# A language-model forward pass in one kernel: three buffers get other addresses modulo 256 bytes

## The reference

```python
def swiglu(x, w_gate, w_up, w_down):
    return (jax.nn.silu(x @ w_gate) * (x @ w_up)) @ w_down
# layer 0: rms_norm, w_in, RWKV-7 recurrence beside sparse attention, w_out, network 0
# layer 1: network 1, then gated linear attention beside forgetting attention, network 2
# layer 2: network 3, then attention over a latent with a top-64 choice, network 4
# then a last rms_norm
```

## The kernel before

| buffer | rounded operands in it | start mod 256, before | after |
|---|---|---|---|
| x, xn | | 128 | 128 |
| uT, yT | uT_h, uT_l | 64 | 128 |
| ffb | h_r | 128 | 128 |
| inh | in_h | 128 | 192 |
| ring | ring_r | 128 | 192 |
| cst (constants), misc | | 128 | 192 |
| wk | w_gu, w_dn, even_h, odd_h, out_h | 128 | 192 |

## Time and profile before

### The profile page before, as it was taken

How to read it: one execution, slowest core, us unless ns; L and a number is a source line. 1 busy time by engine, 2 the same in 40 slices (tenths; PEclk the granted TensorE clock), 3 DMA queues, 4 the chain that set the end, 5 groups by cost and what they waited for, 6 DMA issues and landing times. The chain is left out here.

```text
span 1418.8 us, 25483 instructions
## 1 busy us (share of the span) xinstructions
PE 1390.2 (98%) x10044; PEld 1289.4 (91%) x10044; DVE 945.5 (67%) x1539; ACT 690.5 (49%) x1107; POOL 82.7 (6%) x137
## 2 busy tenths in 40 slices
PE   8999999999999999999999999999999999999997
PEld 7897988999989999999989999999999988899997
DVE  5778567766668666667467666676665676676665
ACT  6764446443354344376654443443443756643342
POOL 1030010000020000010000000100000123000000
PEclk9999999999999999999999999999999999999999
DMA  9344006654536555523356544365555423465540
GB/s 362 141 154 186 2 6 239 219 190 177 184 128 223 192 201 184 179 95 133 130 195 224 201 181 178 134 223 190 202 185 179 149 90 135 178 223 182 191 160 30
DMA packets 33069, 239.47 MB, mean 169 GB/s; under 512 B 6864, under 2 KB 13280, under 8 KB 14304
## 3 DMA queue, kind: packets, MB, share of 16 engines
q1 hardware_dynamic: 30320, 234.84, 45.7%
q10 hardware_dynamic: 2672, 3.58, 0.7%
HBM read 236.15 MB, written 2.25 MB: 168 GB/s over the span
## 5 line engine op out<-in xcount | busy, mean ns | idle before, releaser
L501 PE MATMUL ps<-uT_h,w_gu 128*128 128x256 f32 x3520 | 618.4, 281 | 2.5 <-ACT uT_h L1319 2.5
L501 PEld LDWEIGHTS ps<-uT_h,w_gu 128*128 128x128 f32 x3520 | 538.4, 188 | 12.6 <-issue 5.1
L501 PE MATMUL ps<-uT_l,w_gu 128*128 128x256 f32 x1760 | 482.0, 281 | 0.0
L501 PEld LDWEIGHTS ps<-uT_l,w_gu 128*128 128x128 f32 x1760 | 331.7, 192 | 0.0
L501 PE MATMUL ps<-w_dn,h_r 128*128 128x512 f32 x1320 | 317.9, 390 | 0.4 <-DVE h_r L2073 0.3
L1371 ACT CAST w_gu<-ring 128x2048 fp32r<-128x2048 f32 x110 | 210.0, 1909 | 155.4 <-PE ps L501 154.4
L501 PEld LDWEIGHTS ps<-w_dn,h_r 128*128 128x128 f32 x1320 | 239.8, 188 | 45.2 <-issue 1.8
L2031 DVE TENSOR_TENSOR w_gu<-ring,w_gu 128x2048 fp32r<-128x2048 f32 x110 | 252.1, 2292 | 35.4 <-ACT w_gu L1371 35.4
L2064 DVE TENSOR_TENSOR us<-ps,bc 128x256 f32<-128x256 f32 x110 | 46.5, 423 | 201.9 <-PE ps L501 201.9
L1384 ACT ACTIVATE wk<-wk 128x256 f32<-128x256 f32 x110 | 46.0, 418 | 266.5 <-DVE wk L2062 266.4
L1377 ACT CAST w_dn<-ring 128x1024 fp32r<-128x1024 f32 x110 | 115.8, 1053 | 75.7 <-PE ps L501 75.5
(11 more groups left out here) (398 smaller groups left out, 1695.7 us busy)
## 6 DMA issues: line engine op xcount, KB each, us to landing
ring<-wstream SPq DMA_DIRECT2D x144, 1536.0 KB, 6.5
cst<-consts_in SPq DMA_DIRECT2D x1, 2185.0 KB, 13.7
wk<-t_row ACTq DMA_DIRECT2D x1, 2048.0 KB, 8.1
wk<-masks_in SPq DMA_DIRECT2D x1, 1216.0 KB, 24.2
x<-x_in SPq DMA_DIRECT2D x2, 512.0 KB, 5.0
ring<-wstream SPq DMA_DIRECT2D x1, 1024.0 KB, 9.1
inh<-gains ACTq DMA_DIRECT2D x2, 512.0 KB, 9.8
tri_blocks<-wk SPq DMA_DIRECT2D x3, 256.0 KB, 2.8
```

Source lines behind the costliest of these rows:

```text
L501: return pe.matmul(o, l, r, start=start, stop=stop, skip_group_check=True)
```

## The change

Buffers get other places. The pad of 192 bytes ahead of uT goes; ffb moves from behind the ring to behind yT; a pad of 64 bytes stands ahead of inh in place of the one of 64 bytes that stood there. All buffers from inh on thus change their start modulo 256 by +64, and so do uT and yT. No instruction, loop, wait or transfer is added or removed.

```diff
         x = sb("x", [P, TT, D])
         xn = sb("xn", [P, TT, D])
-        sb("phase_up", [P, 48])
         uT = sb("uT", [P, KC, T])
         yT = sb("yT", [P, KC, T])
-        sb("phase_down", [P, 16])
+        ffb = sb("ffb", [P, 4, T])
+        sb("phase_inh", [P, 16])
         inh = sb("inh", [P, KC * 3 * P])
         gb = inh[:, 0:2 * D].rearrange("p (a b) -> p a b", b=D)
         sb("gate_r", [P, 2 * KC * 24])
         ring = sb("ring", [P, RING, SLOT])
-        ffb = sb("ffb", [P, 4, T])
         cst = sb("cst", [P, NCONST])
```

## The result

The changed kernel takes 1402.56 us (median of 4 runs, 1401.33 to 1405.57) against 1418.22 us (4 runs, 1417.04 to 1421.44): ratio 0.9889, 95% interval 0.9876 to 0.9902. It is 15.7 us faster, where 4 us slower was forecast. The profiled execution has a span of 1401.6 us against 1418.8.

A forecast was written before the change was run, and what follows sets the result against it. TensorE, busy for 98% of the span, was taken to bound the kernel. The down product's 3.0 us plus 0.6 us for dear first matmuls, 3.6 us on the median 1418.63, gave 1422.2 us, range 1399 to 1430.

The forecast's parts named there:

- The down product's price: Down product's 1,320 512-column matmuls: relation going from 0 to -64 costs 2.25 ns each, 3.0 us.
- the 0.6 for first matmuls that stay a little dear: Down product: first matmuls after each switch stay dear, some 5 ns a step over 110 steps, 0.6 us.
- Both entries are slow. So I leave gate/up at 117.7 ns, cost nothing.: Gate/up after the down product: two handovers from -64 to +64 read slow, so spacing stays 117.7 ns, 0 us.
- gate/up goes fast: Gate/up product: the new down product leaves it at fast spacing, 21.6 us back, 1400.6 us; chance 0.20.
- The fear that absolute position counts: Gate/up's 5,280 matmuls: if absolute position modulo 256, not the difference, counts, each nanosecond is 5.3 us.
- nothing changes: TensorE's two reads: they do not disturb each other, so the time stays 1418.6 us; chance 0.15.
- pays in full: Down product: all 12 matmuls at 232 ns each step, +7.0 us, 1425.6 us; chance 0.20 including other losses.
- The small pairs at 0: Ten groups, 312 matmuls, pairing a staying buffer with a moving one: at most 1.3 us either way, taken as 0.

The follow-up runs named there:

- e13: e6 with the last down matmul cut from 512 to 384 columns; 1412.53 us, ratio 0.9956.
- e12: e6 with the last down matmul cut from 512 to 256 columns; 1388.23 us, ratio 0.9782.
- e1: Changed kernel's activation and weight positions modulo 256, but inner values at 192, so the down product is at relation 0 again; 1418.17 us, ratio 0.9994.
- e2: Activations and weights where the kernel before has them modulo 256, inner values at 64, so the down product is at relation -64; 1405.82 us, ratio 0.9916.
- e5: Kernel before, no address moved; all down matmuls take a uT_h tile as stationary operand, relation -64; 1402.77 us, ratio 0.9892.
- e6: Kernel before, no address moved; only the last of 12 down matmuls takes a uT_h tile as stationary operand, relation -64; 1402.35 us, ratio 0.9889.
- e8: Changed kernel with inner values at 160, so the down product is at relation -32 (stationary minus moving start, modulo 256); 23 us slower than the changed kernel.
- e9: Changed kernel with inner values at 96, so the down product is at relation -96; down matmuls at 233 ns, total time not in the text.
- g0: Against the changed kernel, activations and weights both at 128, inner values 64: gate/up at relation 0, down kept at -64; gate/up 119.9 ns, total not given.
- e11: Against the changed kernel, activations 64, weights 192, inner values 128: gate/up at relation 128, down kept at -64; gate/up 119.9 ns, total not given.
- e3: Changed kernel with inner values at 0, so the down product's relation d is +64; gate/up steps alternate 5.46 and 5.65 us, total not given.
- e4: Changed kernel with inner values at 64, so the down product's relation d is 128; gate/up steps alternate fast and slow, total not given.

## Why the prediction was wrong

- **The down product's price** was right to 0.1 ns. The output projections' rows gave 228.9 ns and the pattern 229, 232, 226; the changed kernel's down product has 228.8 in that pattern and 2.75 us per step, as forecast. The term was 3.0 + 0.6 = 3.6 us and came to 2.7; the 0.6 for first matmuls that stay a little dear did not come.
- **"Both entries are slow. So I leave gate/up at 117.7 ns, cost nothing."** This is the step that failed: the term of 5,280 gate/up matmuls, put at nothing, was -17.7 us. It carried over two handovers, behind 384 and 256 columns, to one behind the down product's 512. In the changed kernel those same two places are still slow: 23 matmuls take 641.26 - 638.56 = 2.70 us and 22 take 1103.38 - 1100.79 = 2.59, 117.4 and 117.7 ns, as these lines of its timeline show, while behind the down product all is fast:

```profile
638.56 0.28 PE L500 MATMUL ps<-uT_h,even_h 128*128 128x256 f32 x1
...
641.26 0.28 PE L500 MATMUL ps<-uT_l,even_h 128*128 128x256 f32 x1
...
1100.79 0.28 PE L500 MATMUL ps<-uT_h,odd_h 128*128 128x256 f32 x1
...
1103.38 0.28 PE L500 MATMUL ps<-uT_h,ring_r 128*128 128x256 f32 x1
```

  So the rows were read rightly and did not bear on the case. For the 384 columns e13 shows it: they hand over otherwise than 512 at equal relations. For the 256 columns e12 shows that the width is not the reason, and the reason stays open. The rows that did bear on it were the earlier trace rows: a down product at relation 0 had been seen to turn fast into slow. That put the old relation under suspicion, and a chance of 0.20 for the way out was low. It was no proof either: of the five other relations behind which the product at 64 was run, two left it fast (-64, -96), two every second time (64, 128) and one slow (-32).
- **The rival "gate/up goes fast"** is what happened. Its price, 21.6 us for all 5,280 at 4.1 ns, was somewhat high: 17.7 came. In the steady steps the difference is 3.9 ns, since the first five matmuls of each step are at 118, 117, 118, 122 and 118 ns before 113.3 sets in; and of the 22 steps of a network the last 19 gained (4,560 matmuls, 17.8 us in all), while the first two of all five networks took 58.4 us before and 58.7 after. Its time, 1400.6, was 2.0 under the measured one. The range from 1399 held the measured time only because it had been stretched to take in this rival.
- **The fear that absolute position counts** was unfounded at the two positions tried (e1, e2).
- **The rival "nothing changes"** is refuted: e5 and e6 change only which bytes TensorE's stationary reads take, and the time moves by 15 us. By the Trainium skill, page "SBUF — State Buffer", section "SBUF: two separate sides", contention on the engine side comes from the port pair that VectorE and GpSimd share alone, and PE waits on no one. Taken as a forecast for this change it fails; whether another engine's accesses ever slow TensorE no run here shows, nor what it is in its two reads that costs the time.
- **The rival "pays in full"** (232 ns) did not come here, but e8 and e9 show 233 ns, more than its bound.
- **The small pairs at 0**: nothing, as forecast. The 2.2 us by which the other matmuls fell are the clock's 2.9 less 0.7 at the beginning.

## What to carry to other kernels

When a stream of matmuls on a busy TensorE runs at two spacings for the same shape and addresses, price the slow one over all of its matmuls (here 5,280 x 3.9 ns is more than 1% of the time), and look at what the product just ahead of it reads: one matmul can set the spacing of the 48 behind it. The relation of the starts of the two operands is a free parameter worth a sweep with pads, each product's together with its neighbour's, since no rule found here (equal relations, the farthest one, halfway values) foretold the best pair. A handover read from the trace is evidence only for the same widths on both sides and the same matmuls ahead of it. And before two traces are compared to the microsecond, the granted clock of both has to be looked at: here it made 2.9 of the 17.2 us.

## What the runs showed of the hardware that was not expected

- The spacing of 256-column fp32r matmuls has lasting values of 113.3 and 117.7 ns at relation 64, and 119.9 ns at 0 and 128 (g0, e11, both behind a down product at -64), with the clock granted at 1.00 in these stretches; 512 columns have 226.7 to 233.4 ns.
- Relation 0 is the cleanest for 512 columns (226.7 ns in steady steps before) and among the worst for 256 (119.9 in g0).
- The choice between the two values has a memory that passes through 12 matmuls: with d = 64 or 128 (e3, e4) it alternates from step to step.
- A shift of 32 bytes matters as much as one of 64: d = -32 against -64 is 23 us (e8 against the changed kernel).
